# A hybrid decoder layer on one core: the gate projection of the second convolution half by seven half-sized products, attention units and weight sums placed anew, and more of the output projection ahead of two router steps

## The reference, cut to what matters

```python
h = rmsnorm(x, attn_norm_w)
xin, bg, cg, q, k, v, g_conv, g_attn = split(h @ w_in)      # widths 1024 1024 1024 1024 128 128 1024 1024
y_conv = bg * causal_depthwise_conv3(cg * xin)
y_attn = sliding_window_attention(rmsnorm(q), rmsnorm(k), v)  # window 128, bias table, sinks
x = x + (sigmoid(g_conv) * y_conv + sigmoid(g_attn) * y_attn) @ w_out
h2 = rmsnorm(x, ffn_norm_w)
x = x + moe(h2)       # router, top 4 of 32 experts, up 1024 -> 2048, clamped SwiGLU, down 1024 -> 1024
```

## Time and profile before

| | us |
|---|---|
| three runs | 1154.15, 1155.16, 1157.01 |
| median | 1155.16 |
| the profiled execution | 1155.1 |
| its span | 1153.2 |
| PE busy, share of the span | 1100.5, 95% |
| DVE, ACT, POOL busy | 440.8, 183.7, 82.8 |
| bytes read from HBM | 439.78 MB |

### The profile page before, as it was taken

How to read it: one execution, slowest core, us unless ns; L and a number is a source line. 1 busy time by engine, 2 the same in 40 slices (tenths; PEclk the granted TensorE clock), 3 DMA queues, 4 the chain that set the end, 5 groups by cost and what they waited for, 6 DMA issues and landing times.

```text
span 1153.2 us, 14712 instructions
## 1 busy us (share of the span) xinstructions
PE 1100.5 (95%) x5895; PEld 494.2 (43%) x5895; DVE 440.8 (38%) x877; ACT 183.7 (16%) x388; POOL 82.8 (7%) x149
## 2 busy tenths in 40 slices
PE   9999999999999999999999999999999999999997
PEld 6678899453333333333333333333333333333332
DVE  4876775752353132332323232323232323232322
ACT  2123331220231111010101010101010101010101
POOL 1775033000000000000000000000000000000000
PEclk9999999999999999999999999999999999999999
DMA  9965439989999999999999999999999999999996
GB/s 318 327 194 130 151 98 300 399 317 431 424 419 426 421 430 429 435 432 430 429 435 433 431 429 435 433 429 431 435 432 429 432 434 432 429 433 434 425 423 280
DMA packets 52819, 444.34 MB, mean 385 GB/s; under 512 B 13036, under 2 KB 19596, under 8 KB 35868
## 3 DMA queue, kind: packets, MB, share of 16 engines
q1 hardware_dynamic: 46712, 436.13, 90.8%
q0 software_dynamic: 5216, 7.03, 2.4%
q10 hardware_dynamic: 852, 0.64, 0.2%
HBM read 439.78 MB, written 2.37 MB: 383 GB/s over the span
## 4 chain that ended last, share of the span: by engine, by line
PE 54%; DMA 38%; POOL 3%; DVE 3%; ACT 1%; issue 1%; SPq 0%; DVEq 0%; ACTq 0%; POOLq 0%
PE pA L1960 29%; DMA ring<-in_w_up 21%; PE pB L1960 18%; DMA ring<-in_w_down 10%; PE pM L1960 6%; DMA area<-in_w_up 5%; PE pM L1963 1%; DMA hn<-in_cache_v_win 1%; POOL keys L952 1%; DMA ring<-in_w_in 1%; PE pA L1963 1%; DMA out<-area 0%; POOL out L960 0%; POOL area L931 0%; POOL conv_row L937 0%
## 5 line engine op out<-in xcount | busy, mean ns | idle before, releaser
L1960 PE MATMUL pA<-ring,hn 128*64 128x512 f32 x1536 | 352.6, 602 | 23.4 <-DMA ring<-in_w_up 23.4
L1960 PEld LDWEIGHTS pA<-ring,hn 128*64 128x64 f32 x1536 | 105.3, 137 | 219.2 <-issue 185.5
L1960 PE MATMUL pB<-ring,area 128*64 128x512 f32 (+2 forms) x784 | 171.5, 591 | 6.6 <-DMA ring<-in_w_down 5.8
L1960 PE MATMUL pB<-area,ring 128*128 128x264 f32 (+2 forms) x928 | 148.5, 350 | 2.2 <-ACT tmp L1080 0.8
L1960 PEld LDWEIGHTS pB<-area,ring 128*128 128x128 f32 (+1 forms) x928 | 120.4, 175 | 27.7 <-issue 4.3
L1960 PE MATMUL pA<-area,hn 128*64 128x512 f32 x512 | 119.3, 609 | 10.4 <-DMA area<-in_w_up 10.4
L1960 PEld LDWEIGHTS pB<-ring,area 128*64 128x64 f32 (+2 forms) x784 | 58.6, 136 | 101.2 <-issue 87.8
L1812 DVE TENSOR_TENSOR x<-pM,x 128x512 f32<-128x512 f32 x60 | 40.1, 692 | 147.3 <-PE pM L1960 147.2
L1183 ACT ACTIVATE area<-area 128x512 f32<-128x512 f32 x30 | 18.9, 631 | 385.2 <-DVE area L1795 385.2
L1727 DVE COPY conv_row<-pM 128x512 f32<-128x512 f32 x30 | 20.6, 686 | 146.4 <-PE pM L1960 146.4
L1960 PEld LDWEIGHTS pA<-area,hn 128*64 128x64 f32 x512 | 36.1, 140 | 74.6 <-issue 59.8
(11 more groups left out here) (335 smaller groups left out, 933.9 us busy)
## 6 DMA issues: line engine op xcount, KB each, us to landing
ring<-in_w_up SPq DMA_DIRECT2D x36, 4096.0 KB, 29.8
ring<-in_w_down SPq DMA_DIRECT2D x18, 4096.0 KB, 29.1
area<-in_w_up SPq DMA_DIRECT2D x12, 4096.0 KB, 30.2
ring<-in_w_up SPq DMA_DIRECT2D x17, 2048.0 KB, 14.6
area<-in_w_down SPq DMA_DIRECT2D x6, 4096.0 KB, 30.0
ring<-in_w_in SPq DMA_DIRECT2D x22, 1024.0 KB, 11.2
ring<-in_w_up SPq DMA_DIRECT2D x14, 1024.0 KB, 9.3
ring<-in_w_down SPq DMA_DIRECT2D x13, 1024.0 KB, 25.9
```

Of the source, the lines that this page charges most:

```text
L1960: return pe.matmul(out, w, m, start=start, stop=stop, skip_group_check=True)
```

## The change

Chunk 7 (cg, second half) joins `SEVEN`. Its products are not gated: ACT copies product 0 (t1) and c11, DVE writes c22, c12 and c21 straight into `cx`. It gets a ring place for its sums, which shifts the places of the chunks before it by one and their `before` with them: chunk 8 is now loaded when PE begins chunk 5 (it was chunk 4), chunk 9 when PE begins chunk 6 (it was chunk 5). The steps of units 1 to 3, of the splits, of the sums and of the last `sides` are placed anew. The two-block turns of units 1 and 2 are cut in two, the second transpose at `SECOND_TURNS`. In `BRANCH` one more contraction tile stands ahead of `groups` and one more ahead of `count` 0, and one fewer behind.

```diff
-SEVEN = (6, 9, 10, 11, 12)
+SEVEN = (6, 7, 9, 10, 11, 12)
...
-UNIT_STEPS = [(11, 12, 12, 13, 13, 18, 19), (18, 18, 19, 20, 21, 27, 28),
-              (26, 27, 28, 29, 30, slot(9, 2), slot(9, 4)),
-              (slot(9, 3), slot(9, 4), slot(9, 5), slot(10, 0), slot(10, 2), slot(10, 6), slot(11, 1))]
-SPLIT_STEPS = [slot(9, 4), slot(9, 6), slot(10, 1)]
-CONV_STEP = slot(10, 1)
-SIDE_STEPS = [20, 21, slot(6, 2), slot(6, 3), 33]
-SUM_STEPS = {6: (19, 20, slot(6, 0), slot(6, 1)), 9: (slot(6, 5), 26, 26, 28), 10: (29, 29, 30, 31),
+UNIT_STEPS = [(11, 12, 12, 13, 13, 18, 19),
+              (18, 18, 19, 19, 20, slot(6, 5), slot(7, 3)),
+              (slot(7, 0), slot(7, 0), slot(7, 1), slot(7, 2), 30, slot(9, 3), slot(9, 5)),
+              (slot(9, 3), slot(9, 4), slot(9, 5), slot(10, 0), slot(10, 2), slot(11, 1), slot(11, 3))]
+SECOND_TURNS = (slot(7, 0), slot(9, 3))
+SPLIT_STEPS = [slot(9, 6), slot(10, 1), slot(10, 4)]
+CONV_STEP = slot(10, 2)
+SIDE_STEPS = [20, 21, slot(6, 2), slot(6, 3), slot(9, 0)]
+SUM_STEPS = {6: (19, 20, slot(6, 0), slot(6, 1)),
+             7: (slot(6, 4), slot(6, 6), slot(7, 2), slot(7, 3)),
+             9: (slot(7, 5), slot(7, 6), slot(7, 6), 30),
+             10: (31, slot(9, 0), slot(9, 1), slot(9, 2)),
              11: (slot(10, 0), slot(10, 1), slot(10, 3), slot(10, 4)),
              12: (slot(11, 2), slot(11, 3), slot(12, 1), slot(12, 2))}
...
+    for n, step in enumerate(SECOND_TURNS):
+        after[step].append(("turn", len(UNITS) + 1 + n))
...
-          ("s_split", 0), ("out", (1, 0)), ("x_cols", 2), ("rms", 0), ("part", (0, 0, 5)), ("groups", 0), ("x_cols", 3),
-          ("logits", 0), ("part", (0, 5, KT)), ("half", 0), ("part", (1, 0, 3)), ("count", 0), ("part", (1, 3, 6)),
+          ("s_split", 0), ("out", (1, 0)), ("x_cols", 2), ("rms", 0), ("part", (0, 0, 6)), ("groups", 0), ("x_cols", 3),
+          ("logits", 0), ("part", (0, 6, KT)), ("half", 0), ("part", (1, 0, 4)), ("count", 0), ("part", (1, 4, 6)),
...
+                    elif s == 2 and (c, "c11") in ACT_DONE and not gated:
+                        act.wait_ge(tile_full, FULL[c, 2])
+                        nc.scalar.activation(quarter(cx[:, :, 2:], c, "c11"), pairs_of(bank_x), ACT.Copy).then_inc(tile_free_act, 1)
...
+                plain = TILES[2 + 4 * (c - 1)][0] == "cg"
...
+                def place_of(name, g):
+                    return quarter(cx[:, :, 2:], c, name) if plain else g
...
-                    read("c22", c_, w_, bank_u)
+                    read("c22", place_of("c22", c_), w_, bank_u)
...
-                    for b in range(UNITS[a][0] + 1):
-                        ins = V.transpose(probT[:, b].rearrange("p h q -> p (h q)"), stage[b])
-                    ins.then_inc(probT_ready, 1)
+                    ins = V.transpose(probT[:, 0].rearrange("p h q -> p (h q)"), stage[0])
+                    if UNITS[a][0] == 0:
+                        ins.then_inc(probT_ready, 1)
+                elif what == "turn":
+                    V.transpose(probT[:, 1].rearrange("p h q -> p (h q)"), stage[1]).then_inc(probT_ready, 1)
```

More of the change, by code:

```diff
@@ L304, in counts @@
             GATED_BEFORE[c] = g
-            gated = TILES[2 + 4 * (c - 1)][0] != "bg"
+            kind = TILES[2 + 4 * (c - 1)][0]
+            gated = kind in ("gc", "ga")
             for s in range(7):
@@ L309, in counts @@
             for name in ("r1", "c11", "w", "c22", "c12", "c21"):
-                if name != "c11" or not gated:
+                if name != "c11" or kind == "bg":
                     d += 1
@@ L313, in counts @@
             for name in ("t1", "c11", "c22", "c12", "c21"):
-                if name == "t1" or gated:
+                if name == "t1" or gated or name == "c11" and kind == "cg":
                     a += 1
@@ L325 @@
 counts()
+AFTER_XIN = [c for c in SEVEN if STEPS.index(("slot", (c, 0))) > STEPS.index(("sides", 4))]
 def seven_before(u):
@@ L1309, in seven @@
                 gated = (c, "c22") in ACT_DONE
+                plain = TILES[2 + 4 * (c - 1)][0] == "cg"
                 def read(name, out, a, b):
                     V.tensor_tensor(out, a, pairs_of(b), ALU.add).then_inc(tile_free_dve, 1)
+                def place_of(name, g):
+                    return quarter(cx[:, :, 2:], c, name) if plain else g
                 def times(name, g):
+                    if plain:
+                        return
                     dve.wait_ge(tile_free_dve, DVE_READ[c, name])
@@ L1322, in seven @@
                     return
-                if s != 2 or not gated:
+                if s != 2 or not (gated or plain):
                     dve.wait_ge(tile_full, FULL[c, s])
@@ L1329, in seven @@
                     read("r1", r1, t1, bank_y)
-                elif s == 2 and not gated:
+                elif s == 2 and not (gated or plain):
                     out = quarter(yc, c, "c11")
@@ L1340, in seven @@
                 elif s == 5:
-                    read("c12", w_, w_, bank_v)
+                    read("c12", place_of("c12", w_), w_, bank_v)
                     if gated:
@@ L1348, in seven @@
                         finish(c, "c12")
-                    read("c21", r1, r1, bank_u)
+                    read("c21", place_of("c21", r1), r1, bank_u)
                     if not gated:
@@ L1549, in _ @@
                     ins.then_inc(prob_ready, 1)
-                elif what == "turn":
+                elif what == "turn" and a < len(UNITS):
                     dve.wait_ge(prob_moved, MOVED[a])
@@ L1983, in product @@
                 w, m, b, first = ((a11, b11, bank_x, True), (s2, side2, bank_y, True), (a12, b21, bank_x, False),
-                                  (s1, side1, bank_y, False), (s3, side3[c > SEVEN[0]], bank_u, True), (s4, b22, bank_v, True),
+                                  (s1, side1, bank_y, False), (s3, side3[c in AFTER_XIN], bank_u, True), (s4, b22, bank_v, True),
                                   (a22, side4, bank_u, False))[s]
@@ L2008, in product @@
                     pe.wait_ge(sums_ready, 4 * SEVEN.index(c) + 3)
-                    pe.wait_ge(h_ready, KT + (3 if c == SEVEN[0] else 5))
-                    if opening:
+                    pe.wait_ge(h_ready, KT + (5 if c in AFTER_XIN else 3))
+                    if UNITS_BEFORE[c]:
                         pe.wait_ge(prob_biased, UNITS_BEFORE[c])
-                    else:
+                    if not opening:
                         pe.wait_ge(tile_free_dve, DVE_READ[c - 1, "c21"])
```

## The result

| | before | after |
|---|---|---|
| median of 8 runs each (lowest to highest) | 1155.58 (1154.15 to 1157.01) | 1162.29 (1158.66 to 1164.91) |
| the profiled execution, its span | 1155.1, 1153.2 | 1161.39, 1159.5 |
| PE busy; mean granted clock of the span | 1100.5; 0.993 | 1103.7; 0.989 |

The ratio is 1.0055, its 95% interval 1.0045 to 1.0065. The median is 6.7 us above before's, where 3.2 less was forecast, and 6.2 above the range. PE is busy longer, though the change takes work from it.

A forecast was written before the change was run, and what follows sets the result against it. PE was taken to bound the kernel until about 238 us, the expert weight stream after that. Terms of 1.8 + 0.82 + 0.22 + 0.38 = 3.2 us took 1155.1 to 1151.9 us, range 1150.3 to 1156.1.

The forecast's parts named there:

- What bounds the kernel: Until about 238 us PE is the bound; a microsecond it saves there is a microsecond of the end.
- The sum: All gains together, 3.2 us off the profiled 1155.1, giving 1151.9 us; chance 0.50.
- chunk 7 by products: Chunk 7 on PE: seven products of 1.8 us replace four tiles of 3.6, 1.8 us less.
- unit 1's norm: Product 2 of chunk 6: norm one step earlier removes PE's 0.82 us wait for ACT's copy t1.
- unit 3's values: Chunk 11: values move from product 1 to product 3, removing PE's 0.22 us wait ahead of them.
- `BRANCH`: At `groups`: one more contraction tile ahead covers PE's wait for DVE, 0.38 us less.
- Queues: SP queue: unit 1's moves behind chunk 9's load, landing at 112.5 to 113 us, costed at nothing.
- the first rival: DVE's first transpose waits for unit 1's late moves, PE loses 5.2 us, 1157.1; chance 0.14 shared with another rival.
- unit 3's turn: DVE's turn ahead of unit 3's values: it and its moves stay where they are in time.
- DVE's dues: DVE's 7.0 us of added work, mostly chunks 6 and 7, meets every due time by about half a microsecond; cost 0.
- Chunk 8's and 9's later loads: Loads now at PE's chunks 5 and 6, long ahead of their use at 130 and 128 us.

The follow-up runs named there:

- e1: The changed kernel with unit 1's moves issued ahead of chunk 9's load; median 1154.42 us, ratio to the kernel before 0.9993.
- e3: The changed kernel with the convolution rows' transpose one product earlier, as in the kernel before; median 1158.34 us, ratio to the kernel before 1.0023.
- e4: The changed kernel with unit 1's moves ahead of chunk 9's load and the convolution rows one product earlier; median 1152.14 us, ratio 0.9973.
- e10: The kernel before with only the change's steps for unit 1's exp and norm and its `BRANCH`; median 1153.64 us, ratio 0.9981.
- e6: The kernel before with only the loads of chunks 8 and 9 put one chunk later; median 1155.08 us, ratio 0.9998.
- e5: e3 with 24 matmuls of no use filling PE's wait ahead of unit 2's scores; median 1157.10 us, ratio to the kernel before 1.0015.
- e2: The changed kernel with unit 1's first transpose two products later, moves still behind the load; median 1158.86 us, ratio 1.0029.

## Why the prediction was wrong

**What bounds the kernel: right.** In every kernel the end went with PE's way to j = 6 to within 1.3 us, in both directions: +6.1 and +6.3 in after, -2.1 and -2.3 in e1, +2.6 and +2.6 in e3, -4.1 and -2.8 in e4 (j = 6, then the span, against before).

**The sum: right, a little small.** e4 has all of the change's parts with nothing in their way. By starts of rows, e4 against before and e10:

| term | forecast | measured |
|---|---|---|
| chunk 7 by products | 1.8 | 1.6: product 4 of chunk 6 to product 0 of chunk 10, 51.72 against 53.36 in e10 |
| unit 1's norm | 0.82 | 1.1: start of chunk 5's last tiles to product 4 of chunk 6, 10.86 against 11.96 |
| unit 3's values | 0.22 | 0.3: product 0 of chunk 10 to the first output, 39.11 against 39.40 |
| `BRANCH` | 0.38 | 0.44: 36.56 against 37.00 |
| sum | 3.2 | 3.4 |

The medians give 3.3. That they come so near to the sum is partly luck: e4's j = 6 is 4.1 us earlier, and its end behind the last scatter is 1.0 longer. A wait is worth a little more than the idle time in its row, since the row counts from a modelled end of the matmul before: 1.1 for 0.82. e4 has another 0.6 us ahead of chunk 6, but kernels without that part of the change show some of it too (chunk 5's last tiles start at 97.57 in before, 97.12 in e6, 96.97 in e4), so I take it for scatter.

**The step that failed is "Queues".** "Unit 1's moves follow chunk 9's load on SP" was costed at nothing, with moves issued to 110.4, landed by 112.5 to 113. They were issued to 113.85 and landed by 118.4. The row for the bound stood in the text, 8.5 us behind the output weights, and the first rival used it: moves at 118.9, PE 5.2 us late. Measured: 118.4 and 5.03. That these agree is half luck, since the rival has the last move issued at 110.4 and 8.5 us under way, and it was issued at 113.85 and 4.6 us under way. I took 2.1 for the sum, although the nearest row for a small move behind a load on the same queue was 8.5. My reason against it, that only the last move counts and it is issued 8 us behind the load, fell twice. SP's issue itself slows down behind the load, so that it was 11 us behind. And when the load was in, the small transfers that had piled up, POOL's moves and the expert biases' loads among them, still filled the engines (the row from 112 to 114 us).

The sentence on the Trainium skill, "DMA: Bandwidth & Descriptors" (Queues, rings and completion order), that a DMA engine takes a ring's descriptors in order, does not carry as far as I took it. From it I concluded that the moves wait only until the load's last packet is taken. The load was in by 111.5, the last move was issued behind that, at 113.85, and still landed at 118.4; what stood ahead of it in SP's queue was the other moves, which I had not counted. The same section says that an engine goes round between the queues packet by packet, so that POOL's moves share the engines with the load. The trace shows them at 5.5 and 6.4 us instead of 2.2 and 1.9. The rules give a direction and no time.

**What the rival left out: the clock.** It priced the wait alone, 1157.1. Behind the wait PE ran at half clock, 3.1 us in the profiled run (6.8 us at the level), 1.5 in e3, none in e5, where PE was kept busy. I had read the row of 40 slices of before as full clock throughout and took that for a constant. It was not one even there. Before's own trace has four spells at half level, at 862, 920, 978 and 1036 us, each behind a wait for expert weights. One of them, the matmuls and then the window (busy times, PEclk, DMA share, GB/s):

```profile
860.71 5.35 PE L1960 MATMUL pA<-ring,hn 128*64 128x512 f32 x16 [1.86 <-DMA ring<-in_w_up]
862.00:864.00 2.00, 2.00 (x6) 0.49 (x4) 0.45 (x1) 0.00 (x0) 0.00 (x0) 0.50 1.10 475
```

Behind a wait as long, 1.87 us at 802.42, a row of the same count and shape takes 3.65 us and the clock stays. In the stream these 1.7 us cost the end nothing, since the weights set the pace: from j = 6 to the last scatter it is 904.0 us in before with four spells, 903.8 in e1 with none and 903.8 in after with five. The spell at 120 us in after cost its time because PE is the bound there.

**The second step that failed is unit 3's turn.** "The turn with its moves stays where it is in time" was wrong: the convolution rows were put one product later. POOL issues their eight outputs ahead of the moves, and so its moves came to stand beside SP's output weights. Values wait 1.8 us where 0.22 were to go. The change of `CONV_STEP` is in the diff and did not appear in my working, against the rule of following every DMA of a step that is moved.

**Put together:** 1155.1 - 3.4 + 5.1 (the wait, from start to start) + 3.0 (the clock) + 1.9 (values: 1.6 and the 0.3 that did not go) = 1161.7. The profiled run took 1161.39. Three costs made 10.0 us. The first sits where my own working had a margin of half a microsecond or less; the other two it did not have at all.

**The rest held.** DVE's dues were all met when the moves were in time: in e1 and e4 no wait for r1, a sum or c21. Chunk 8's and 9's later loads cost PE nothing, and up to 300 us PE waits for no weights in after or in e4.

## What to carry to other kernels

A small DMA whose landing is awaited goes ahead of a big load in the queue, or well clear of it, and that holds for another engine's queue too: behind 2 MiB it landed in 4.5 to 8.9 us instead of 2, and 3 us of distance were not enough (e6). Where a bound from the trace stands near to the case, use it for the sum and not its comfortable neighbour. Where PE is the bound, price a new wait at its length and leave room for the clock behind it: 3.0 and 1.5 us behind waits of 5.0 here. A 9 in a row of slices does not say that the clock is full; look at its mean and at short windows. When an added gain comes back as a loss, look for the order of issue before giving up the gain: here one number in each of two tables turned 6.7 us slower into 3.3 faster.

## What the runs showed of the hardware that I had not expected

- SP took 10.7 us to issue ten moves 0.9 us behind a load of 2 MiB (12.0 in e5), 7.0 with 3 us in between (e6), 6.7 with the load behind them (e1). So a late move is late by issue and by landing.
- POOL's moves, on their own queue, landed in 5.5 and 6.4 us beside the load, 2.2 and 1.9 without. Their issue was no slower, 2.9 us for five in both.
- Behind a wait of 5.0 us the granted clock fell to the 1.2 GHz level for 6.8 us in one execution and 3.4 in another. Behind waits of 1.8 us (after, e1) it did not fall, behind one of 2.15 (e2) it did; in before's stream it fell behind a wait of 1.86 us at 860.71 and not behind one of 1.87 at 802.42. So the length of the wait alone does not tell.
- Matmuls that do nothing, put into the wait, kept the clock up: the way from product 0 of chunk 7 to unit 1's values was 14.5 us with them (e5) and 15.2 without (e3).
- At 112 to 114 us in after the DMA engines were fully taken at 193 GB/s by transfers of 32 and 64 KB, most of whose packets are under 512 bytes, against 432 GB/s in the stream.
- In the stream, where the weights set the pace, spells at half clock cost the end nothing: 903.8 us from j = 6 to the last scatter with none (e1) and with five (after).
